# Second rows of u computed ahead of a weight split, LayerNorm squares paired on POOL, one more shared tap product, last sums loaded by POOL's queue

## The reference

```python
a, b, p, gc, gp = jnp.split(rms_norm(x) @ w_in, IN_SPLITS, axis=-1)
u = a * jax.nn.sigmoid(b)                       # 256 x 512
u = causal_depthwise_conv(u, 31 taps) + dw_b
xc = u - mean(u); var = mean(xc * xc)           # LayerNorm over the 512 channels
yc = silu(xc * rsqrt(var + 1e-5) * ln_g + ln_b) @ w_conv_out
yp = multiscale_pool(p, w_pool) * pool_scale
x = x + (sigmoid(gc) * yc + sigmoid(gp) * yp) @ w_out
...
for e in range(8):                              # layer 1, channel mixer
    y = y + comb[:, e:e + 1] * swiglu(t, w_gate[e], w_up[e], w_down[e])
return rms_norm(x + y, final_norm)
```

## Time and profile before

| | |
|---|---|
| time, median of 3 runs | 1419.75 us (1419.68 to 1420.81) |
| the profiled execution's own time | 1420.94 us |
| its span, first to last instruction | 1419.2 us |
| PE busy | 1405.4 us (99%) |
| DVE busy | 1176.6 us (83%) |
| ACT busy | 985.3 us (69%) |
| POOL busy | 212.8 us (15%) |
| mean granted clock of TensorE | 0.997 |

### The profile page before, as it was taken

The page is one execution under the profiler, slowest core; times in us unless marked ns, Lnnn a source line. Parts: engine busy times, 40 slices in busy tenths (PEclk is TensorE's granted clock), DMA queues, the critical chain, the costliest instruction groups (busy, mean ns, idle before and its releaser), DMA issues.

```text
span 1419.2 us, 18324 instructions
## 1 busy us (share of the span) xinstructions
PE 1405.4 (99%) x6490; PEld 1166.0 (82%) x6490; DVE 1176.6 (83%) x1069; ACT 985.3 (69%) x869; POOL 212.8 (15%) x251
## 2 busy tenths in 40 slices
PE   9999999999999999999999999999999999999997
PEld 7888888888888888888888888888888888888885
DVE  6997544548987998889899898888989889888896
ACT  7765434347765877867867777786786777778675
POOL 6840000005831101001001001000100100100020
PEclk9999999999999999999999999999999999999998
DMA  9656555545548899999999999999999999999992
GB/s 360 213 177 216 181 180 193 191 152 204 171 170 303 287 402 363 370 369 410 375 383 371 390 369 371 388 384 356 409 373 383 370 390 370 368 396 389 363 389 85
DMA packets 197840, 446.45 MB, mean 315 GB/s; under 512 B 8570, under 2 KB 20138, under 8 KB 197792
## 3 DMA queue, kind: packets, MB, share of 16 engines
q1 hardware_dynamic: 192496, 432.57, 80.8%
q0 software_dynamic: 2592, 8.87, 2.3%
q10 hardware_dynamic: 2704, 4.38, 0.9%
HBM read 438.49 MB, written 7.86 MB: 315 GB/s over the span
## 4 chain that ended last, share of the span: by engine, by line
PE 93%; DVE 4%; DMA 1%; ACT 1%; SPq 0%; issue 0%; POOL 0%; ACTq 0%; POOLq 0%
PE bank L1482 29%; PE bank L1484 29%; PE bank L1483 29%; PE bank L1662 2%; DVE bank L1057 2%; DVE w_lo L1008 2%; DMA raw<-in_w_in_dram 1%; PE bank L1540 1%; ACT w_hi L674 1%; PE bank L1829 0%; DMA out_dram<-tokA 0%; SPq L460 0%; PE bank L1624 0%; PE bank L1804 0%; PE bank L1618 0%
## 5 line engine op out<-in xcount | busy, mean ns | idle before, releaser
L1008 DVE TENSOR_TENSOR w_lo<-raw,w_hi 128x2048 fp32r<-128x2048 f32 x256 | 582.8, 2291 | 134.3 <-ACT w_hi L674 134.1
L674 ACT ACTIVATE w_hi<-raw 128x2048 fp32r<-128x2048 f32 x256 | 488.1, 1912 | 200.1 <-PE bank L1484 198.8
L1482 PE MATMUL bank<-w_hi,dT_hi 128*128 128x512 f32 (+1 forms) x756 | 296.3, 392 | 0.0
L1484 PE MATMUL bank<-w_hi,dT_lo 128*128 128x512 f32 (+1 forms) x756 | 293.2, 388 | 0.0
L1483 PE MATMUL bank<-w_lo,dT_hi 128*128 128x512 f32 (+1 forms) x756 | 292.6, 387 | 0.0
L1482 PE MATMUL bank<-w_hi,cT_hi 128*128 128x512 f32 x492 | 194.3, 395 | 0.0
L1484 PE MATMUL bank<-w_hi,cT_lo 128*128 128x512 f32 x492 | 191.7, 390 | 0.0
L1483 PE MATMUL bank<-w_lo,cT_hi 128*128 128x512 f32 x492 | 191.6, 389 | 0.0
L1484 PEld LDWEIGHTS bank<-w_hi,dT_lo 128*128 128x128 f32 x756 | 141.9, 188 | 29.4
L1482 PE MATMUL bank<-w_hi,hT_hi 128*128 128x512 f32 x416 | 164.1, 394 | 1.3 <-DVE hT_lo L1022 1.0
L1482 PEld LDWEIGHTS bank<-w_hi,dT_hi 128*128 128x128 f32 x756 | 142.0, 188 | 28.4
(11 more groups left out here) (260 smaller groups left out, 1859.0 us busy)
## 6 DMA issues: line engine op xcount, KB each, us to landing
raw<-in_moe_w_gate_dram SPq DMA_DIRECT2D x96, 1024.0 KB, 7.5
raw<-in_moe_w_up_dram SPq DMA_DIRECT2D x72, 1024.0 KB, 10.3
raw<-in_moe_w_down_dram SPq DMA_DIRECT2D x72, 1024.0 KB, 9.0
raw<-in_w_in_dram SPq DMA_DIRECT2D x20, 1024.0 KB, 5.7
mix<-in_moe_w_up_dram SPq DMA_DIRECT2D x16, 1024.0 KB, 8.5
gates<-in_moe_w_down_dram SPq DMA_DIRECT2D x16, 1024.0 KB, 11.2
gates<-in_moe_w_up_dram SPq DMA_DIRECT2D x16, 1024.0 KB, 8.7
work<-in_moe_w_down_dram SPq DMA_DIRECT2D x16, 1024.0 KB, 10.9
```

Of the source, the lines that this page charges most:

```text
L674: act.activation(w_hi[split_place(u, seen.item is not None)][:, 0:width], place[slot][:, 0:width], ACT.Copy).then_inc(hi_ready, 1)
L1008: dve.tensor_tensor(w_lo[split][:, 0:width], place[slot][:, 0:width], w_hi[split][:, 0:width].bitcast(F32), ALU.subtract).then_inc(lo_read ...
L1482: nc.tensor.matmul(dst, a_hi, b_hi, start=start, stop=False)
L1484: return nc.tensor.matmul(dst, a_lo, b_hi, start=False, stop=stop)
```

## The change

There are four edits.

1. In layer 0 alone, DVE does four more taps first (12 in place of 8) and then the second rows of u, and only then splits the next unit (number 5). In layer 1 the order stays.
2. `SHARED` goes from 13 to 14: in each layer DVE does one tap less, ACT one product more (its last call goes to 45), and POOL one add more.
3. POOL adds the squares in pairs, block 1 to block 0 and block 3 to block 2, each as one 128x256 addition in place, behind each signal of ACT's squares. PE's matmuls for the variance go from four to two, and each waits for a sum of POOL in place of ACT's square. In POOL's program the two additions stand behind the adds of the convolution and ahead of the scaling of the gates.
4. The two loads of `sums` leave SP's queue and are issued by POOL, behind its indirect fetch of rows. SP's wait for the scatters goes.

```diff
-    SHARED = 13
+    SHARED = 14
...
-            sp.wait_ge(scattered, n_items * 16)
-            for b in range(TB):
-                sp.dma_start(xs[:, b, :], sums[b * P:(b + 1) * P, :]).then_inc(sums_landed, 16)
...
+                for i in range(2):
+                    pool.wait_ge(centred_sq, seen.next(centred_sq))
+                    pair_of = sq[:, 2 * i * S:(2 * i + 1) * S]
+                    pool.tensor_tensor(pair_of, pair_of, sq[:, (2 * i + 1) * S:(2 * i + 2) * S], ALU.add).then_inc(sq_paired, 1)
+
...
+            for b in range(TB):
+                pool.dma_start(xs[:, b, :], sums[b * P:(b + 1) * P, :]).then_inc(sums_landed, 16)
...
-                tap_products(l, 44)
+                tap_products(l, 45)
...
-                conv_taps(8)
-                split_to(U + 6)
-                u_rows(1, M.high)
+                if l:
+                    conv_taps(8)
+                    split_to(U + 6)
+                    u_rows(1, M.high)
+                else:
+                    conv_taps(12)
+                    u_rows(1, M.high)
+                    split_to(U + 6)
...
-                    for c in range(CC):
-                        if c % 2 == 0:
-                            pe.wait_ge(centred_sq, seen.next(centred_sq))
-                        last = nc.tensor.matmul(bank[M.var][:, 0:S], mean_w[:, :], sq[:, c * S:(c + 1) * S], start=c == 0, stop=c == CC - 1)
+                    for c in (0, 2):
+                        pe.wait_ge(sq_paired, seen.next(sq_paired))
+                        last = nc.tensor.matmul(bank[M.var][:, 0:S], mean_w[:, :], sq[:, c * S:(c + 1) * S], start=c == 0, stop=c == 2)
```

More of the change, by code:

```diff
@@ L362, in trunk_kernel @@
         mean_done, centred, centred_sq, var_done = sem("mean_done"), sem("centred"), sem("centred_sq"), sem("var_done")
+        sq_paired = sem("sq_paired")
         std_ready, normed, silu_conv = sem("std_ready"), sem("normed"), sem("silu_conv")
```

## The result

The changed kernel takes 1426.85 us (median of 6 runs, 1425.16 to 1428.85), the kernel before beside it 1419.78 us (6 runs). The ratio is 1.0047, its 95% interval 1.0034 to 1.0060: slower by 7.07 us, where 4.6 were forecast. The profiled execution took 1427.2 us, with a span of 1425.4 us and a mean granted clock of 0.996.

The account below looks back on a forecast made before the run. PE's own stream was taken as the bound. -0.39 + 2.5 + 2.5 = +4.6 us, on 1419.75, gave 1424.3 us, +0.3%; own range 1423.4 to 1425.6, full range 1422.6 to 1426.9; slower 0.87.

Parts of the forecast that it names:

- the full range: Whole kernel: 1422.6 to 1426.9 us, reaching to the case of a falling clock.
- the rival of the falling clock: Behind PE's stall at the variance: 1.2 GHz costs 1.25 us more a layer, total 1426.8 us; chance 0.08.
- What bounds the kernel: PE's stream: it never waits from 84.24 us to the expert loop's end, so an added stall is not won back.
- Edit 1, worth nothing alone: Layer 0, turning of u: PE gains 0.96 us but waits longer at the mean, since DVE's work is unchanged.
- its upper bound: Edits 1 and 2 together: at most 0.96 us gained, should a DVE split lose its delay behind POOL.
- Edit 2, -0.39 us: Layer 0, mean after the convolution: DVE's chain ends 0.39 us earlier and PE gains as much; layer 1 nothing.
- hidden by 0.3 us: Layer 0, convolution: POOL's added operation ends at 83.54; the join of block 3 needs it at about 83.85.
- Edit 3, +2.5 us a layer: Variance: DVE's splits block POOL's pair additions, delaying PE's next slab 2.5 us, including 0.81 us of saved matmuls.
- a sign of being wrong: Profile check: a granted clock under 1.00 at 90 or 400 us would speak against the forecast.
- Downstream of the variance: Behind the statistics: cT, gate scaling and unit 15 come in time, so PE has no second stall.
- Edit 4: End weights: 1 MB of sums among them, 3.3 us, is hidden by 11 us of slack; cost nothing.
- The tail stays: Behind PE's last work: the tail keeps its length.

Follow-up runs that it names:

- experiment 9: Kernel before with edit 1 only (second rows of u ahead of the split in layer 0): 1419.01 us, ratio 0.9995.
- before: The kernel before the change, with none of the four edits: 1419.78 us beside the changed kernel.
- experiment 6: Kernel before with edit 2 only (14 shared taps): 1419.41 us, ratio 0.9993.
- experiment 2: Kernel before with edits 1, 2 and 4, so everything but the pair additions: 1419.39 us, ratio 0.9995.
- experiment 7: Changed kernel with the two pair additions on DVE, between its narrow and its wide split: 1419.53 us, ratio 0.9995 against the kernel before.
- experiment 3: Changed kernel with useless small matmuls filling PE's two waits at the variance: 1423.67 us, ratio 1.0024 against the kernel before.
- after: The changed kernel with all four edits: 1426.85 us, ratio 1.0047 against the kernel before.
- experiment 8: Changed kernel with DVE's splits held until both pair sums are done and half of POOL's gate scaling moved ahead of the additions: 1421.82 us, ratio 1.0010.
- experiment 5: Kernel before with edit 4 only (sums loaded by POOL's queue): 1420.55 us, ratio 1.0001.
- experiment 1: Kernel before with edit 3 only (squares paired on POOL): 1426.02 us, ratio 1.0040.
- 10: Kernel before with one unused single-column operation added behind ACT's last product of each mixer: 1419.72 us, ratio 0.9997.
- experiment 4: Changed kernel with DVE waiting for both pair sums before its two splits: 1429.3 us, ratio 1.0061 against the kernel before.

## Why the prediction was right, and where it fell short

**The forecast as a whole.** Slower was right. The forecast's own range, 1423.4 to 1425.6 us, was missed; 1426.85 lies in the full range, to 1426.9, only because that takes in the rival of the falling clock. (The chances given for slower add up to 0.88, not 0.87.)

**What bounds the kernel: right.** Shifts of PE stay where they arise. The +6.83 us at the end of layer 1's slab is still +7.02 at PE's last matmul, 1000 us later.

**Edit 1, worth nothing alone: wrong in the step, inside its bounds.** The prediction took DVE's work up to the mean as fixed. Experiment 9 shows it 0.76 us shorter, because two splits lost their delays behind POOL's adds (2.76 to 2.28 us, and 2.72 to 2.44). That is the condition which the prediction had set on its upper bound, 0.96 us for edits 1 and 2. The median of experiment 9 is 0.94 us under before, which its interval doesn't tell from nothing.

**Edit 2, -0.39 us: near.** Alone (experiment 6) it brings the windows of layer 0 forward by 0.41 us; with edits 1 and 4 (experiment 2) it is 0.43, and in the changed kernel 0.49. The step "hidden by 0.3 us" for POOL's added operation failed once edit 1 was there too: DVE came 1.2 us earlier (last tap at 82.53), and the join then waited 0.71 us for POOL. That is why 0.76 and 0.39 don't add up.

**Edit 3, +2.5 us a layer: mechanism right, size 0.4 us high.** The prediction of 1.4 to 1.8 and about 2.7 us for the additions, and about 2.9 us for the split, met 1.58, 2.77 and 2.81 us. With the clock's part in the variance matmuls of layer 0 taken off (they take 0.66 us before the slab, 0.35 in layer 1), the path costs +2.1 us in each layer. The missing 0.35 us are three small terms: the wide split ended 0.12 us sooner after its predecessor's start than reckoned (3.95 for 4.07 us); the second addition ended 0.59 us behind that split, as the add of the earlier trace rows did with 0.60, where the sum had 0.74; and the last sum's matmul took 0.35 us before the slab, where the sum had 0.41. The waits were forecast at 3.3 us a layer and are 2.5: PE's delay of 2.1 and the saved matmuls make 2.9, and the records of the matmuls run on past the point where the next one could start, so the rest isn't counted as waiting. The Trainium skill, page "SBUF — State Buffer", section "Who interferes with whom", says that the one that comes second is blocked for the whole of the first instruction; the trace agrees, both additions ending 0.59 us behind the split beside them, and with the additions on DVE (experiment 7) the loss is gone.

**The clock: this is the step that failed.** The sum held only the path, and the falling clock stood among the rivals at 0.08 and 1.25 us a layer. It fell in both layers, which the prediction had named as a sign of being wrong. By the stages it costs 0.31 + 1.23 us in layer 0 and 1.63 in layer 1, 3.2 us together, and experiment 3 measures 3.2 to 3.5 us. The rival's time, 1426.8, met the measured one by luck: its path was 0.4 us a layer too long, its clock 0.3 to 0.4 us a layer too short, and it held neither the shorter tail (-0.8 us) nor the 0.9 us between the spans and the medians. The argument had compared the coming gap of 2.5 us with a wait of 1.6 us that left the clock at the top, and given that row more weight than it bears: it is PE's wait for its very first matmul. And the low level does stand in the trace of before, from about 1411.4 us on, 2.0 us behind the end of PE's last matmul:

```profile
1.57 2.50 PE L1670 MATMUL bank<-ident 128*128 128x128 f32 x10 [1.57 <-POOL ident L538]
...
1409.05 0.39 PE L1484 MATMUL bank<-hT_hi,cT_lo 128*128 128x512 f32 x1
```
```profile
1412.00:1413.00 1.00, 0.00 (x0) 0.00 (x0) 0.75 (x1) 0.72 (x1) 0.17 (x1) 0.50 0.01 2
```

The gap was not even one gap, but 0.5 us, the passes of one matmul, and 2.0 us. The Trainium skill, page "TensorE: Matmul & The Clock Gate", Part 1, says that an idle PE is throttled to half its rate; here the granted clock of 0.50 agrees.

**Downstream of the variance: right.** No wait of PE at cT, the gates or unit 15 appears in after. The cover was not wide, though: experiment 8 shows that 1.6 us more on DVE come out at the gates as a wait of 1.7 us a layer.

**Edit 4: right**, by experiment 5.

**The tail stays: wrong by 0.82 us, in the other direction.** ACT's gap ahead of the final norm went from 2.17 to 0.82 us. It was not the sums (experiment 5: 2.25), the order of the rows (9: 2.34) or the pairs (1: 2.32). One operation more in each mixer of ACT's program does it, a product (6) or an idle one (10). These are readings of one profiled execution each. The eleven times of experiment 9 fall into two groups, seven up to 1419.30 us and four from 1420.04, and its trace is of the upper one; whether the executions of the lower group had the gap too is not shown. What "issue" stands for there is not settled.

**The total.** -0.5 for edits 1 and 2, +2.1 and +2.1 for the path, +3.2 for the clock, +0.1 unassigned, and -0.8 in the tail give the +6.2 us of the spans. The medians say 0.9 us more, within the interval. It stays open why edit 3 alone gave 1426.02 and all four edits 1426.85, though the other three give 1419.39: the spread that the low stretch brings, 1425.2 to 1429.0, covers it, with 5 and 6 runs.

## What to carry to other kernels

When an engine is given a step in PE's path, look at what the engine that can block it (here DVE for POOL, with two operands in SBUF each) has queued at that moment: an addition of 0.7 us took up to 2.8, and holding the neighbour back only moved the clash to the next pair. Price a stall of an otherwise full PE with the clock behind it, which here put 1.5 to 1.6 us on top of each path that was 2.1 us longer, and test that price by filling the stall with small matmuls. Taking matmuls out gains nothing where the values behind them are late: here the 0.43 us a layer that PE won at the variance with the pairs on DVE were lost again at the gates.

## What was not expected of the hardware

- Waits of 0.5 and 2.0 us, with the matmul passes of the first sum between them, were followed by the low clock in both layers of after and in both of experiment 1, for somewhat over 3 us, and once for almost 7. The length of a wait alone does not decide it. In experiment 4 PE waited 1.90 us for the gates in each layer; the clock fell behind the wait of layer 0 and stayed at the top behind that of layer 1:

```profile
110.15 1.09 PE L1551 MATMUL bank<-ident,gates 128*128 128x128 f32 x8 [1.90 <-DVE gates L1212]
...
423.93 1.09 PE L1551 MATMUL bank<-ident,gates 128*128 128x128 f32 x8 [1.90 <-DVE gates L1212]
```
```profile
112.00:114.00 2.00, 2.00 (x6) 1.52 (x6) 2.00 (x4) 0.38 (x2) 0.00 (x0) 0.50 0.08 31
424.00:426.00 2.00, 2.00 (x13) 1.81 (x14) 1.76 (x5) 1.21 (x4) 0.88 (x7) 1.00 0.97 374
```

  Behind the waits of 1.69 and 1.66 us of experiment 8 it stayed at the top too. What parts the two cases is open.

- Between two splits of DVE that follow each other directly, POOL's waiting addition gets in: the first addition ended 1.81 us behind the start of the narrow split (1.22 us long), and the wide split took 2.81 in place of 2.28 us.
- A gap of ACT near the end of the program goes with how many instructions its program has: 2.17 to 2.34 us in the four profiles without an added one, 0.81 to 0.82 us in the nine with one more in each mixer (one profiled execution each).
